# A trunk of two layers on one Trainium2 core: seven projection tiles taken from x instead of from the normed h, and four rows of the first modulation made by TensorE

## What is computed

```python
for l in range(2):
    mod = silu(c) @ w_ada[l] + b_ada[l]              # 6 parts of 1024
    sh1, sc1, g1, sh2, sc2, g2 = split(mod, 6)
    h = rms_norm(x, norm1_g[l]) * (1 + sc1) + sh1    # rms over the 1024 columns of a token
    proj = h @ w_in[l]                               # q, k, v of three attentions, forget gates, merge gates
    x = x + g1 * mixers(proj, ...)
    h = rms_norm(x, norm2_g[l]) * (1 + sc2) + sh2
    x = x + g2 * peer_ffn(h, ...)                    # 128 x 128 experts, all computed densely
```

## Time and profile before

| | |
|---|---|
| runs | 2206.87, 2209.35, 2210.81 us, median 2209.35 |
| profiled execution | 2206.84 us, its span 2204.7 us |
| busy in the span | TensorE 98%, VectorE 76%, ScalarE 56%, GpSimd 11% |
| granted clock of TensorE, mean | 0.992 of 2.4 GHz |
| HBM read | 424.99 MB, 193 GB/s over the span |

### The profile page before, as it was taken

One profiled execution on the slowest core, in us unless ns is written; L12 is line 12 of the kernel. 1 busy time (PEld: TensorE's weight loads), 2 busy tenths in 40 slices (PEclk: granted clock), 3 DMA queues, 4 the chain that ended last, 5 costly groups with the idle time before them and its releaser, 6 DMA issues.

```text
span 2204.7 us, 42946 instructions
## 1 busy us (share of the span) xinstructions
PE 2157.1 (98%) x14992; PEld 1993.0 (90%) x14992; DVE 1674.5 (76%) x3205; ACT 1227.9 (56%) x2152; POOL 250.1 (11%) x298
## 2 busy tenths in 40 slices
PE   5999999999999999999999999999999999999999
PEld 4889999999999988888888899999999999888887
DVE  6787777889589956777567868788885998567765
ACT  3656565444577745544555565744445776554454
POOL 0210000000156400000002100000002662000000
PEclk7999999999999999999999999999999999999999
DMA  8465654555533367777555666455555334588765
GB/s 330 172 210 212 211 191 166 185 183 175 184 129 110 111 198 257 253 257 233 190 191 173 221 214 213 158 182 184 178 188 165 113 114 142 191 277 256 255 211 171
DMA packets 114863, 427.28 MB, mean 194 GB/s; under 512 B 12752, under 2 KB 13008, under 8 KB 113616
## 3 DMA queue, kind: packets, MB, share of 16 engines
q1 hardware_dynamic: 114768, 426.08, 57.6%
HBM read 424.99 MB, written 1.05 MB: 193 GB/s over the span
## 4 chain that ended last, share of the span: by engine, by line
PE 93%; DVE 3%; DMA 1%; issue 1%; ACT 1%; POOL 0%; SPq 0%; ACTq 0%; DVEq 0%; POOLq 0%
PE pj L1350 18%; PE pj L1352 17%; PE pj L1351 17%; PE wk L1350 10%; PE wk L1351 10%; PE wk L1352 10%; PE wk L1673 5%; DMA arena<-in_front 1%; PE wk L1474 1%; DVE lo L823 1%; PE wk L1413 1%; PE wk L1467 1%; PE wk L1451 0%; PE wk L1610 0%; ACT hi L483 0%
## 5 line engine op out<-in xcount | busy, mean ns | idle before, releaser
L823 DVE TENSOR_TENSOR lo<-raw,hi 128x1024 fp32r<-128x1024 f32 x683 | 845.4, 1240 | 445.2 <-ACT hi L483 440.4
L483 ACT ACTIVATE hi<-raw 128x1024 fp32r<-128x1024 f32 x683 | 721.3, 1057 | 461.2 <-PE wk L1352 342.3
L1350 PE MATMUL pj<-mov_hi,hi 128*128 128x256 f32 x3120 | 903.9, 290 | 25.5 <-DVE mov_lo L870 21.1
L1352 PE MATMUL pj<-mov_hi,lo 128*128 128x256 f32 x3120 | 884.9, 284 | 0.0
L1351 PE MATMUL pj<-mov_lo,hi 128*128 128x256 f32 x3120 | 884.5, 283 | 0.0
L1350 PEld LDWEIGHTS pj<-mov_hi,hi 128*128 128x128 f32 x3120 | 599.9, 192 | 36.4 <-issue 30.8
L1351 PEld LDWEIGHTS pj<-mov_lo,hi 128*128 128x128 f32 x3120 | 600.0, 192 | 0.2
L1352 PEld LDWEIGHTS pj<-mov_hi,lo 128*128 128x128 f32 x3120 | 599.3, 192 | 0.0
L1350 PE MATMUL wk<-hi,mov_hi 128*128 128x512 f32 x1024 | 398.5, 389 | 1.9 <-DVE mov_lo L1300 1.9
L1352 PE MATMUL wk<-hi,mov_lo 128*128 128x512 f32 x1024 | 398.4, 389 | 0.0
L1351 PE MATMUL wk<-lo,mov_hi 128*128 128x512 f32 x1024 | 398.3, 389 | 0.0
(11 more groups left out here) (199 smaller groups left out, 1718.5 us busy)
## 6 DMA issues: line engine op xcount, KB each, us to landing
raw<-in_stream SPq DMA_DIRECT2D x684, 512.0 KB, 3.4
arena<-in_ada SPq DMA_DIRECT2D x72, 512.0 KB, 4.9
onehot_a<-in_ada SPq DMA_DIRECT2D x24, 512.0 KB, 4.3
arena<-in_front SPq DMA_DIRECT2D x4, 2048.0 KB, 18.1
arena<-in_taba SPq DMA_DIRECT2D x2, 1536.0 KB, 18.2
arena<-in_keys SPq DMA_DIRECT2D x2, 1024.0 KB, 5.8
x<-in_xT SPq DMA_DIRECT2D x1, 1024.0 KB, 4.9
arena<-in_mix SPq DMA_DIRECT2D x2, 512.0 KB, 14.9
```

The source lines that it names most:

```text
L483: nc.scalar.activation(hi[j % SPLIT][:, :], raw[j % RAW][:, :], ACT.Copy).then_inc(hi_done, 1)
L823: nc.vector.tensor_tensor(lo[j % SPLIT][:, :], raw[j % RAW][:, :], hi[j % SPLIT][:, :].bitcast(f32), ALU.subtract).then_inc(lo_done, 1)
L1350: pe.matmul(out, w_h, m_h, start=first, stop=False)
L1352: return pe.matmul(out, w_l, m_h, start=False, stop=last)
```

## The change

Tiles 0 to 6 of each layer are projected from u1 = x * amp (with two columns of the shift), as the query stage does with u2. VectorE multiplies the result by rstd1 (`u_scaled`), ScalarE adds the shift's column as a bias in place. Tiles 0 and 1 run side by side, chunk by chunk, in the two banks. The normed h1 is made during tiles 0 to 6 (H1_AT) and used from tile 7 on. In layer 0 the 16 front rows come in eight transfers of two, the scale rows (8 to 15) first, x before the last two; rows 0 to 3 come turned and are made by TensorE (8 products of one output column each), the other 12 by VectorE. For layer 1 scales and shift columns are made inside the down stage, squares, u1 and its rests right behind x. The core of the diff:

```diff
+H1_AT = ((0, 1, 2), (3,), (4,), (5,), (6,), (7,), (), ())
+N_U = 7
+FRONT = ((8, 0), (9, 0), (10, 0), (0, 1), (11, 0), (1, 1), (12, 0), (2, 1), (13, 0), (3, 1), (14, 0), (15, 0), (4, 0), (5, 0),
+         (6, 0), (7, 0))
...
         @block.sync
-            sp.dma_start(x[:, :, :], x_dram).then_inc(setup_loaded, 16)
-            sp.dma_start(par_all[:, :, :], par_dram).then_inc(setup_loaded, 16)
-            for j in range(AHEAD):
+            sp.dma_start(par_all[:, :, :], par_dram).then_inc(par_loaded, 16)
+            for j in range(2):
                 sp.dma_start(raw[j][:, :], stream[j]).then_inc(raw_loaded[j], 16)
-            for j in range(4):
-                f = slice(j * ADA_FIRST // 4, (j + 1) * ADA_FIRST // 4)
+            for j in range(ADA_FIRST // 2):
+                if j == 6:
+                    sp.dma_start(x[:, :, :], x_dram).then_inc(x_loaded, 16)
+                f = slice(2 * j, 2 * j + 2)
                 sp.dma_start(ada_front[:, f, :], front_dram[:, f, :]).then_inc(front_loaded[j], 16)
...
         @block.scalar
+            def first_norm(l, link):
+                for k in range(KC):
+                    act.wait_ge(x_ready, l * KC + (k + 1))
+                    nc.scalar.activation(sq[:, k, :], x[:, k, :], ACT.Square).then_inc(sq_ready, 1)
+                act.wait_ge(amp_ready, l + 1)
+                for k in range(KC):
+                    nc.scalar.activation(u1[:, 0, k, 0:SEQ], x[:, k, :], ACT.Copy, scale=amp[:, 0, k:k + 1])\
+                        .then_inc(u_head, 1)
+                act.wait_ge(ss_ready, 2 * l + 1)
+                link(nc.scalar.activation(rstd1, wk[:, 0, 0:SEQ], ACT.Ln, bias=eps, scale=1.0 / D))
+                nc.scalar.activation(rstd1, rstd1, ACT.Exp, scale=-0.5).then_inc(rstd_ready, 1)
...
                 def evict(t):
+                    if t < N_U:
+                        act.wait_ge(out_free, l * OUTS + (t + 1 + 2))
+                        nc.scalar.activation(projT[:, t, :], projT[:, t, :], ACT.Identity, bias=cols[:, t, 0:1])\
+                            .then_inc(u_out, 1)
+                        return
                     act.wait_ge(tile_done, L0 + (t + 1 + SPLIT))
...
                 for t in range(DENSE):
                     head(L0 + (t + AHEAD), t + AHEAD)
+                    if t < N_U:
+                        for n in H1_AT[t]:
+                            norm_head(0, h1, n)
                     if t == NORM_A:
-                        act.wait_ge(out_free, l * OUTS + (KA + 1 + 2))
+                        act.wait_ge(u_out, l * N_U + KA + 1)
...
         @block.vector
+            front(0, 12)
+            dve.wait_ge(par_loaded, 16)
+            dve.wait_ge(late_used, KC)
+            scales(0, slink)
+            dve.wait_ge(x_loaded, 16)
+            for k in range(4):
+                u_rest(0, 0, u1, k)
+            front(12, 14)
+            for k in range(4, 6):
+                u_rest(0, 0, u1, k)
+            front(14, 16)
+            for k in range(6, KC):
+                u_rest(0, 0, u1, k)
+            dve.wait_ge(front_done, N_TURNED)
...
+            shift_columns(u1, MS1, slink).then_inc(u_ready, KC)
...
+                def u_scaled(t):
+                    dve.wait_ge(tile_done, L0 + (t + 1 + SPLIT))
+                    nc.vector.tensor_tensor(projT[:, t, :], pj[t % 2][:, 0:SEQ], rstd1, ALU.mult)
+                    nc.vector.tensor_copy(cols[:, t, :], pj[t % 2][:, SEQ:COLS]).then_inc(out_free, 1)
...
                 for t in range(DENSE):
+                    if 0 < t <= N_U:
+                        u_scaled(t - 1)
...
                     rest_of(L0 + (t + AHEAD), t + AHEAD)
+                    if t < N_U:
+                        if t == 0:
+                            dve.wait_ge(rstd_ready, 2 * l + 1)
+                        else:
+                            for n in H1_AT[t - 1]:
+                                norm_rest(0, h1, n)
+                        for n in H1_AT[t]:
+                            norm_scaled(0, h1, rstd1, n)
...
+                dve.wait_ge(late_used, (l + 1) * ADA_LATE + ADA_FIRST)
+                link(nc.vector.tensor_tensor(mod[:, MG2:MS1], mod[:, MG2:MS1], par[:, MG2:MS1], ALU.add))
+                if l + 1 < DEPTH:
+                    scales(l + 1, link)
+                    link(nc.vector.tensor_tensor(mod[:, MS1:MC1], mod[:, MS1:MC1], par_all[:, l + 1, MS1:MC1], ALU.add))
+                    link(shift_columns(u1, MS1, link))
                 with dve.Fori((LATE_AT + 3 * ADA_LATE) // 4, NKEYS // 4 - 1) as i:
...
                         mod[:, MG2 + k:MG2 + k + 1], x[:, k, :], ALU.mult, ALU.add).then_inc(x_ready, 1)
+                if l + 1 < DEPTH:
+                    for k in range(KC):
+                        u_rest(l + 1, 0, u1, k).then_inc(u_ready, 1)
                 dve.wait_ge(x_ready, l * KC + 2 * KC)
                 dve.sem_inc(arena_free, 1)
...
         @block.tensor
+            for n, (tile, turned) in enumerate(FRONT):
+                if turned:
+                    pe.wait_ge(front_loaded[n // 2], 16)
+                    for k in range(KC):
+                        last = pe.matmul(wk[:, 1, tile:tile + 1], ada_front[:, n, k * P:(k + 1) * P], c_silu[:, k:k + 1],
+                                         start=k == 0, stop=k == KC - 1)
+                    last.then_inc(front_done, 1)
...
-                for t in range(DENSE):
+                for t in range(2):
+                    pe.wait_ge(lo_done, L0 + t + 1)
+                    pe.wait_ge(out_free, l * OUTS + t + 1)
+                for k in range(KC):
+                    pe.wait_ge(u_ready, 2 * KC * l + k + 1)
+                    for t in range(2):
+                        last = product(pj[t][:, 0:COLS], *chunk(t, k), u1[:, 0, k, :], u1[:, 1, k, :], k == 0, k == KC - 1)
+                        if k == KC - 1:
+                            last.then_inc(tile_done, 1)
+                for t in range(2, N_U):
+                    early_pieces(t)
+                    project_u(L0 + t, t, t, t % 2, u1, None).then_inc(tile_done, 1)
+                for t in range(N_U, DENSE):
                     early_pieces(t)
```

More of the change, by code:

```diff
@@ L91 @@
 MIX_AT = (KC, 0, 4)
+H1_AT = ((0, 1, 2), (3,), (4,), (5,), (6,), (7,), (), ())
+N_U = 7
+FRONT = ((8, 0), (9, 0), (10, 0), (0, 1), (11, 0), (1, 1), (12, 0), (2, 1), (13, 0), (3, 1), (14, 0), (15, 0), (4, 0), (5, 0),
+         (6, 0), (7, 0))
+N_TURNED = sum(turned for _, turned in FRONT)
 H_AT = ((), (0, 1), (2,), (3,), (4,), (5,), (6, 7), ())
@@ L155, in trunk @@
         with nc.sbuf_tensor("u_skip", [P, U_AT[1], SEQ], f32), nc.sbuf_tensor("u2", [P, 2, KC, COLS], f32r) as u2:
+            pass
+        with nc.sbuf_tensor("u_skip1", [P, U_AT[0], SEQ], f32), nc.sbuf_tensor("u1", [P, 2, KC, COLS], f32r) as u1:
             pass
@@ L252, in trunk @@
         c_row = sem("c_row")
-        front_loaded = [sem(f"front_loaded{i}") for i in range(4)]
+        front_loaded = [sem(f"front_loaded{i}") for i in range(ADA_FIRST // 2)]
         ada_loaded = [sem(f"ada_loaded{i}") for i in range(ADA_SLOTS)]
@@ L520, in norm_head @@
                                          bias=mod[:, shift:shift + 1]).then_inc(h_hi, 1)
[L523 to L528, removed]
-                    norm_head(0, sq, k)
                 def evict(t):
@@ L836, in _, with scales @@
             dve.sem_inc(arena_free, 1)
[L837 removed]
+            dve.sem_inc(x_ready, KC)
+            for j in range(2):
                 rest_of(j, j)
[L839 removed]
             nc.vector.tensor_copy(picks[:, :], const[:, C_PICK:C_PICK + HEADS])
[L841 to L847 removed]
+            def scales(l, link):
+                par = par_all[:, l, :]
+                link(nc.vector.tensor_tensor(mod[:, MC1:MC1 + KC], mod[:, MC1:MC1 + KC], par[:, MC1:MC1 + KC], ALU.add))
+                nc.vector.scalar_tensor_tensor(amp[:, 0, :], mod[:, MC1:MC1 + KC], 1.0, par[:, PG1:PG1 + KC],
+                                               ALU.add, ALU.mult).then_inc(amp_ready, 1)
+                for n, g in ((0, PQA), (1, PQB)):
+                    link(nc.vector.tensor_scalar(gain[:, n:n + 1], par[:, g:g + 1], HD ** -0.5, None, ALU.mult))
@@ new lines, in _, with front @@
+            dve.wait_ge(c_row, 1)
+            def front(first, last):
+                for n in range(first, last):
+                    if n % 2 == 0:
+                        dve.wait_ge(front_loaded[n // 2], 16)
+                    tile, turned = FRONT[n]
+                    if not turned:
+                        modulate(ada_front[:, n, :], mod[:, MS1 + tile:MS1 + tile + 1], late_used)
+            front(0, 12)
+            dve.wait_ge(par_loaded, 16)
+            dve.wait_ge(late_used, KC)
@@ L849, in _ @@
+            nc.vector.tensor_tensor(mod[:, MS1:at], wk[:, 1, 0:N_TURNED], par_all[:, 0, MS1:at], ALU.add)
+            slink(nc.vector.tensor_tensor(mod[:, at:end], mod[:, at:end], par_all[:, 0, at:end], ALU.add))
```

(5 more changed lines are left out.)

92 lines of the change are left out of this document (44 added, 48 removed).

## The result

The changed kernel takes 2230.23 us (median of 4 runs, 2229.26 to 2230.44) against 2208.43 for the kernel before, run beside it: ratio 1.0097, 95% interval 1.0079 to 1.0114, that is 21.8 us slower. The forecast was 2230.0. The profiled execution has a span of 2228.4 us (2204.7 before), 23.7 more; the profiled execution of before is one of the fastest of its kernel, as the prediction noted.

The account below looks back on a forecast made before the run. TensorE bounds the kernel, 93% of the span. Layer 0 +11.5, layer 1 +10.9, end -0.2 give +22.2 on the profiled 2206.8: 2229.0; forecast 2230 us, allowing for that run being low. Range 2216 to 2237.

Parts of the forecast that it names:

- The ring: Tiles 1 to 6: VectorE, ScalarE and TensorE wait on each other, 3.95 us a round against 2.88 per tile.
- the first round: First turn through the three engines, with three norm_rest: 4.75 us.
- The wait for Square: Before tile 6's norms, TensorE waits some 6 us for ScalarE's Square, which starts 4.5 us after u_scaled(4).
- The clock: Behind the 6 us idle before tile 6's norms, TensorE runs at half rate: 2.7 us more per layer.
- The rival in which the clock falls in the ring's small waits: Tiles at half rate take 5.8 us, 1.8 more for three tiles in two layers: 2240 us; chance 0.05.
- The other rival, that the clock holds through that wait: No clock loss behind the wait before tile 6: 5.4 us less, 2223 to 2226 us; chance 0.12.
- Layer 0: Start through tile 6: first product at 35.8, tile 6 ending at 74.1 instead of 62.6, +11.5 us.
- Turned rows: Four front rows on TensorE before layer 0: 3 us each, 12 in all, hidden in its idle time.
- Layer 1: Start through tile 6: tile 6 ending at 1157.8 instead of 1146.9, +10.9 us.
- The wait of head(4): Layer 1: ScalarE asks for raw tile 4 at 1125.5 and waits until it lands at 1128.6.
- The gain of the early start: Layer 1: first product at 1118.2 without idle and at full clock, tile 1 done at 1124.0, gaining 6.3 us.
- The 0.2 of the small addition: A small VectorE addition leaves the end of both layers, saving 0.2 us each.

Follow-up runs that it names:

- e1: Changed kernel with ScalarE's eviction of tiles 0 to 6 moved one loop later, behind head; 2225.64 us, ratio 1.0082 to the kernel before.
- e2: As e1, with norm_head also one loop and norm_rest two loops later than norm_scaled; 2210.71 us, ratio 1.0011 to the kernel before.
- e5: Changed kernel with 50 unread products on TensorE ahead of the wait before tile 6's norms; 2226.21 us, ratio 1.0080 to the kernel before.
- e3: Changed kernel with only arena_free given ahead of the eight rests of u; 2227.1 us, ratio 1.0087 to the kernel before.
- e6: Changed kernel with all sixteen front rows made by VectorE, none turned, same transfer order; 2231.59 us, ratio 1.0102 to the kernel before.
- e8: As e2, with raw tiles 4 to 6 issued on SP ahead of the arena_free wait and tables; 2203.85 us, ratio 0.9974; again 2203.61 us, 0.9977.
- e4: Changed kernel with the changes of e2 and e3 together; 2205.59 us, ratio 0.9985 to the kernel before.
- e10: As e8, with 30 unread products on TensorE behind layer 0's squares, before its first tile; 2203.31 us, ratio 0.9975 to the kernel before.

## Why the prediction was right

**The ring: right, in length to 0.01 us, with a second way of the same length that the prediction did not list.** 3.95 was forecast and 3.94 to 3.95 measured, the first round 4.75 as forecast. The prediction led the round through u_scaled's two operations and the eviction that waits for them (0.52 + 0.41). The chain of waits of the profile after leads it through norm_head, which waits for norm_scaled, and then the eviction (0.52 + 0.42 + 0.40 in the fences above, and head, rest and norm_rest 1.07 + 1.15 + 0.39): 3.95 as well, since norm_head takes the place of u_scaled, which stands one operation later on VectorE. e1 bears the sum out by one term, e2 by cutting it. The cut needed norm_head moved too, as this reading says; the prediction's own list would have stopped at the eviction, which is e1 and leaves 17 us. The trace alone would not have told the two ways apart: the copy of the columns ends at 50.07 (49.92 + 0.15), 0.05 before the eviction starts. That the way through norm_head binds by itself is shown by e1, where the way through u_scaled is gone and 3.54 remain: the length of the ring that the prediction had read in the query stage. No run moves norm_head alone.

**The wait for Square: right.** 4.5 us from u_scaled(4) to Square were forecast, 4.47 measured (61.42 to 65.89), and TensorE waits 6.1. The waits before it are smaller than forecast, 0.83 us for about 1.1, and in layer 1, where the clock was low, those of tiles 4 and 5 are missing.

**The clock: right, a little large.** 2.7 us was forecast for each layer; against e5 the changed kernel loses 2.8 and 2.3, and e3 and e6 lose 2.1 and 2.3 in layer 0. Most of it is in the norms: 4.60 us, 2.40 in e5. The rival in which the clock falls in the ring's small waits is out: it is 0.99 in 42 to 60 us, through waits of 0.9 us on average. So what the Trainium skill tells of another kernel (TensorE: Matmul & The Clock Gate, "A second HAM failure mode: psum-queue depth-cycling"), a clock that goes back and forth through small idle pieces between groups of products, does not show here at waits of 0.3 to 1.6 us. The clock fell behind the long ones, 6.1 us in both layers and 5.84 in layer 1. The other rival, that the clock holds through that wait, fell too.

**Layer 0: +12.8, forecast +11.5.** First product 36.59 for 35.8: the first pair of rows was there at 10.02, not 9.3, the next ones 2.49 apart for 2.45, and x at 24.86 for 24.0. u_scaled(0) came at 44.84, 0.9 later than forecast, and everything behind it moved along; the remaining 0.4 is in norms and tile 6. Both are no larger than what two kernels with the same layer 0 differ by: by e3's 73.97 layer 0 costs 11.3.

**Turned rows: right that they are hidden, their price above the value taken.** 13.8 us for four, 3.45 each, for 3 taken (between bounds of 0 and 6.47). e6 shows that they buy nothing: VectorE, with one row of a pair instead of two, waits longer for the next pair.

**Layer 1: +12.0, forecast +10.9.** The wait of head(4) was forecast at 3.1 us (asked at 1125.5, landed at 1128.6) and measured at 4.12, which is most of the difference. The term that was too small is the transfer's: the queue issued raw tile 4 at 1134.31, 7.9 us behind the start of x (8.2 forecast), and ScalarE had it 8.25 us later, not 6.7, which was the median of six transfers; in e2, e3 and e4 it took 8.5. e3 prices what hangs on it at 3.8, where the prediction's bound had 3. The gain of the early start is in the trace (u_scaled(0) 11.0 behind the start of x), and e8 shows what it is worth when nothing takes it back: 3.3 us from x to tile 6, not 6.3. From the first u_scaled to that of tile 6 even the cut order takes 19.0 us (1126.51 to 1145.54), against 16.6 from tile 1's eviction to tile 6's before (tiles 0 and 1 end together in the new order); in it TensorE waits 0.85 us before tile 2 and 1.15 before the norms. So of the 5.7 us by which the first two tiles are out earlier behind x, 2.4 go again by tile 6.

**Behind tile 6: 1.0 us came back that the sum did not have.** 0.9 of it is a gap of TensorE at 1217.65 in the kernel before that the changed one has not; the profile names no releaser for it, and why it is there stays open. The 0.2 of the small addition, claimed per layer, is not visible in layer 0, where tile 6 and x moved by the same 12.7.

**Sum.** By the spans +23.7 for +22.2 forecast: the two layers were 2.3 short together, 1.0 came back, and the 0.2 of the small addition wasn't there to be taken off. By the medians +21.8. The prediction's sum was 2229.0, and 1.0 was added for the spread of before; that this meets the measured 2230.23 within 0.3 us is luck. The mechanism is right, and the terms of its sum are right to 1.6 us or better, the transfer of raw tile 4 being the worst.

## What to carry to other kernels

Follow one round of a loop through the in-order engines, station by station, and compare its length with the work of the slowest engine: here neither ScalarE nor VectorE was full (1.8 and 2.4 us of work against 2.88 for a tile on TensorE), and the round still took 3.95. To cut such a ring, let each engine take up in loop t what the other began in loop t-1. Then ask what the faster loop will want earlier, because a transfer that stands behind a wait which nobody needed before is the next thing in its way (e2 to e8: 7 us). With both mended, the same change is 0.25% faster than the kernel before instead of 1% slower. Marks of single executions can differ by more than a term is worth (1.4 us here for the same instructions), so compare distances within one execution before positions in two.

## What the runs showed of the hardware

- The 32 f32 products with a one-column output (four rows of eight) stand in the trace as 64 instructions that overlap: each lasts 352 ns, beside a weight load of 332, and all take 13.8 us, so one begins every 0.22 us and a product costs 0.43.
- The granted clock was 0.50 throughout 13 to 26 us in the changed kernel, in e5, e8 (twice) and e10, and 1.00 in e1 to e4, with the same instructions on TensorE; the 64 took 13.8 us at either. The changed kernel and e3 don't differ before the end of layer 0 and show both levels, so the level didn't matter to these products, and what set it no run shows. It did matter behind them: the squares took 6.7 us in the changed kernel and 5.5 in e1, and from the first product to u_scaled(0) it is 8.1 to 8.3 us where the level had been 0.50 and 7.1 to 7.2 where it had been 1.00 (e10 apart, 5.7).
- At 0.50 TensorE was busy without a gap for 13 us in those rows and the clock did not rise. It rose at the end of the squares, which follow them: in the changed kernel 0.50 in 31 to 32 us, 0.93 in 32 to 33, and 1.00 in 33 to 34, where TensorE was idle already; in 36 to 37 it was back at 0.50. In e10 it is 1.00 from 32 to 33 on, and with 30 fp32r products in that place it stays there.
- The clock was 0.50 in 38 to 40 us, behind 3.8 us or more of idle before the first tile, in every kernel but e10, which idled 0.43 us there. It fell in or behind the waits of 5.3 (e1), 5.8 and 6.1 us, and held through those of 0.3 to 1.6.
